# First loads in pieces, warm-up matmuls, a folded norm from half sums, masks by predicated copy, and the last unit by token half, in a two-block model kernel

## The reference

```python
def rmsnorm(x, g):
    y = x * rsqrt(mean(x * x, -1) + EPS)
    return y * g

def first_block(x, ...):
    for l in range(2):
        x = x + 0.5 * swiglu(rmsnorm(x, g_ffn1[l]), w1_a[l], w3_a[l], w2_a[l])
        x = x + mixer_1(rmsnorm(x, g_mix[l]))        # Fourier, convolution and pooling branches, gated
        x = x + 0.5 * swiglu(rmsnorm(x, g_ffn2[l]), w1_b[l], w3_b[l], w2_b[l])
    return rmsnorm(x, g_final)

def second_block(x, ...):
    for l in range(2):
        x = x + 0.5 * swiglu(rmsnorm(x, ffn1_norm[l]), ...)
        x = x + mixer_2(rmsnorm(x, mix_norm[l]))     # window attention and gated linear attention
        x = x + 0.5 * swiglu(rmsnorm(x, ffn2_norm[l]), ...)
    return x
```

## Time and profile before

| what | value |
|---|---|
| median of 3 runs | 2351.07 us |
| the profiled execution: its time, its span | 2351.17 us, 2349.4 us |
| PE busy | 2321.5 us, 99% |
| DVE busy, ACT busy | 1329.9 us (57%), 1119.6 us (48%) |
| mean granted TensorE clock | 0.999 |
| DMA | 417.06 MB, mean 178 GB/s |

### The profile page before, as it was taken

One profiled execution on the slowest core, in us unless ns is written; L12 is line 12 of the kernel. 1 busy time (PEld: TensorE's weight loads), 2 busy tenths in 40 slices (PEclk: granted clock), 3 DMA queues, 4 the chain that ended last, 5 costly groups with the idle time before them and its releaser, 6 DMA issues.

```text
span 2349.4 us, 26325 instructions
## 1 busy us (share of the span) xinstructions
PE 2321.5 (99%) x10836; PEld 1920.1 (82%) x10836; DVE 1329.9 (57%) x1456; ACT 1119.6 (48%) x1223; POOL 0.2 (0%) x4
## 2 busy tenths in 40 slices
PE   8999999999999999999999999999999999999999
PEld 6887888888888788888788888788888887878887
DVE  5554566555554466554555676755455548576553
ACT  5444444444444444443544664454454447545442
POOL 0000000000000000000000000000000000000000
PEclk9999999999999999999999999999999999999999
DMA  8555455555655455656556543455555555245653
GB/s 266 184 188 209 153 193 182 188 189 175 192 189 178 152 187 180 197 179 206 157 192 204 184 148 113 161 162 181 204 170 186 199 174 179 93 142 162 197 179 126
DMA packets 310268, 417.06 MB, mean 178 GB/s; under 512 B 16610, under 2 KB 201442, under 8 KB 310148
## 3 DMA queue, kind: packets, MB, share of 16 engines
q1 hardware_dynamic: 309860, 415.24, 54.1%
q10 hardware_dynamic: 288, 0.14, 0.0%
HBM read 414.27 MB, written 1.05 MB: 177 GB/s over the span
## 4 chain that ended last, share of the span: by engine, by line
PE 96%; DVE 2%; ACT 1%; issue 1%; DMA 0%; DVEq 0%; ACTq 0%
PE psum L587 30%; PE psum L589 29%; PE psum L588 29%; PE psum L604 3%; PE psum L858 1%; PE psum L684 1%; DVE wlo L1499 0%; ACT whi L1078 0%; PE psum L834 0%; PE psum L701 0%; PE psum L844 0%; PE psum L845 0%; PE psum L825 0%; DMA xt_in<-t_xt_dram 0%; DVE rb L1989 0%
## 5 line engine op out<-in xcount | busy, mean ns | idle before, releaser
L1499 DVE TENSOR_TENSOR wlo<-raw,whi 128x2048 fp32r<-128x2048 f32 (+2 forms) x408 | 882.5, 2183 | 459.3 <-ACT whi L1078 456.9
L1078 ACT ACTIVATE whi<-raw 128x2048 fp32r<-128x2048 f32 (+2 forms) x408 | 734.4, 1828 | 306.4 <-PE psum L589 301.7
L587 PE MATMUL psum<-whi,xt_hi 128*128 128x512 f32 (+1 forms) x2144 | 849.6, 396 | 10.0 <-DVE wlo L2026 10.0
L589 PE MATMUL psum<-whi,xt_lo 128*128 128x512 f32 (+1 forms) x2144 | 834.5, 389 | 0.0
L588 PE MATMUL psum<-wlo,xt_hi 128*128 128x512 f32 (+1 forms) x2144 | 833.4, 389 | 0.0
L587 PEld LDWEIGHTS psum<-whi,xt_hi 128*128 128x128 f32 x2144 | 404.0, 188 | 91.9 <-DVE wlo L2026 10.0
L589 PEld LDWEIGHTS psum<-whi,xt_lo 128*128 128x128 f32 x2144 | 403.3, 188 | 85.0
L588 PEld LDWEIGHTS psum<-wlo,xt_hi 128*128 128x128 f32 x2144 | 404.2, 189 | 79.7 <-issue 1.0
L587 PE MATMUL psum<-whi,ht_hi 128*128 128x512 f32 x704 | 275.3, 391 | 0.0
L589 PE MATMUL psum<-whi,ht_lo 128*128 128x512 f32 x704 | 274.1, 389 | 0.0
L588 PE MATMUL psum<-wlo,ht_hi 128*128 128x512 f32 x704 | 273.9, 389 | 0.0
(11 more groups left out here) (232 smaller groups left out, 1405.3 us busy)
## 6 DMA issues: line engine op xcount, KB each, us to landing
raw<-w_in_dram SPq DMA_DIRECT2D x180, 512.0 KB, 4.5
raw<-w_b_dram SPq DMA_DIRECT2D x128, 512.0 KB, 4.9
raw<-w_a_dram SPq DMA_DIRECT2D x126, 512.0 KB, 4.9
raw<-ffn_w_gate_dram SPq DMA_DIRECT2D x88, 512.0 KB, 4.1
raw<-ffn_w_up_dram SPq DMA_DIRECT2D x88, 512.0 KB, 5.2
raw<-ffn_w_down_dram SPq DMA_DIRECT2D x80, 512.0 KB, 4.7
raw<-w_o_dram SPq DMA_DIRECT2D x16, 512.0 KB, 4.4
raw<-w_proj_b_dram SPq DMA_DIRECT2D x16, 512.0 KB, 4.2
```

The costliest lines, as they stand in the source:

```text
L587: nc.tensor.matmul(pair(p, m)[:, out], hi[:, c, t], whi[:, slot, w], start=first, stop=False)
L589: last = nc.tensor.matmul(pair(p, m)[:, out], lo[:, c, t], whi[:, slot, w], start=False, stop=final)
L1078: nc.scalar.activation(whi[:, u % HL, first:n], raw[:, r, first:n], ACT.Copy).then_inc(hi_done, 1)
L1499: nc.vector.tensor_tensor(wlo[:, u % HL, first:n], raw[:, r, first:n], whi[:, u % HL, first:n], ALU.subtract).then_inc(w_ready, 1)
```

## The change

It has five parts.

1. xt comes in three pieces (chunks 0-1, 2-3, 4-7); the first half of unit 0 is split in two pieces of 512 columns, and PE starts after the first. Ahead of that, ACT runs one small Copy on a tile that DVE sets, and PE runs 16 transposes of `ident` into an unused bank once `ident` is in.
2. The norm between the blocks: x times gfin is kept as `xgf` (`x_scaled`), and the squares of x and of xgf are summed by column half (`final_squares`, results in `fss`), the first half during the last feed-forward of block 1. `final_norm` makes both scales from these sums. x = xgf * rfin is written afterwards. The load of `gfin` is issued in the middle of that feed-forward instead of at its end.
3. The masks: two `copy_predicated` into a zeroed `pg` in place of products and sums; `pg` is set to zero once in each mixer.
4. The last unit by token half (`last_blocks`): all six matmuls of tokens 0-127, then those of 128-255; DVE adds the first half after the semaphore `first_m`.
5. The wait for `ident` is made once, ahead of the warm-up, and not in each `hidden_transposes`.

```diff
+WARM = 16
+FIRST_PARTS = (slice(0, 2), slice(2, 4), slice(4, 8))
...
+                if (e.block, e.lay) == (1, LAYERS - 1) and u0 > 0:
+                    eng.wait_ge(w_used, units(e, u0, HL))
+                    eng.dma_start(gfin[:, :], a["g_final"].rearrange("(a n) -> a n", a=1).partition_broadcast(P)
+                                  ).then_inc(gfin_in, 16)
...
             xt_part(0)
             first_unit(a["w1_a"], a["w3_a"], 0, first_in)
             xt_part(1)
             first_unit(a["w1_a"], a["w3_a"], 1, raw_in[0])
+            xt_part(2)
             gate_up(flat(a["w1_a"]), flat(a["w3_a"]), 4 * P, 0, 1)
...
+            def last_blocks(u, p, split, chunks):
...
+                for m in range(MT):
+                    t = slice(m * P, (m + 1) * P)
+                    for i, c in enumerate(chunks):
+                        w = slice(i * 512, (i + 1) * 512)
+                        nc.tensor.matmul(pair(p, m), hi[:, c, t], whi[:, slot, w], start=False, stop=False)
+                        nc.tensor.matmul(pair(p, m), hi[:, c, t], wlo[:, slot, w], start=False, stop=False)
+                        last = nc.tensor.matmul(pair(p, m), lo[:, c, t], whi[:, slot, w], start=False,
+                                                stop=i == len(chunks) - 1)
+                    last.then_inc(first_m if m == 0 else w_used, 1)
...
             eng.sem_inc(w_used, HL)
+            eng.wait_ge(ident_in, 16)
+            for _ in range(WARM):
+                nc.tensor.transpose(psum[:, 5, 0:P], ident[:, :], ident[:, :])
             eng.wait_ge(first_ready, 1)
             eng.wait_ge(done, e.after(done, ("xt", "ffn0", 0, 0)))
-            blocks(0, 0, 0, XT, (0, 1), True, False, False, ready=False)
+            blocks(0, 0, 0, XT, (0,), True, False, False, ready=False)
+            eng.wait_ge(first_ready, 2)
+            blocks(0, 1, 0, XT, (1,), False, False, False)
...
+            def final_squares(half, scaled):
+
+                cols = slice(512 * half, 512 * half + 512)
+                src, out = (xgf, junk2) if scaled else (x, junk)
+                for m in range(MT):
+                    last = nc.scalar.activation(out[:, m, cols], src[:, m, cols], ACT.Square,
+                                                accum_out=fss[:, scaled, half, m:m + 1])
+                return last
...
                 if stage == "ffn0" and (e.block, e.lay) == (2, 0):
-                    squares("final", out)
                     root("final")
+                    root(stage)
                     split(u0 + 3)
-                    eng.wait_ge(done, e.after(done, ("x2",)))
-                    squares(stage, out)
-                    root(stage)
...
+                if stage == "ffn0" and (e.block, e.lay) == (2, 0):
+                    eng.wait_ge(x_whole, wholes(e))
+                    final_squares(1, 0).then_inc(acted, e.mark(acted, ("ss", "final")))
+                    eng.wait_ge(xgf_done, 2)
+                    final_squares(1, 1).then_inc(acted, e.mark(acted, ("ss", "ffn0")))
+                    x_hi(stage, 1)
...
+                        if next_stage == "ffn0" and (e.block, e.lay) == (1, LAYERS - 1):
+                            final_squares(0, 0)
+                            eng.wait_ge(xgf_done, 1)
+                            final_squares(0, 1)
...
+            def x_scaled(half):
+
+                cols = slice(512 * half, 512 * half + 512)
+                for m in range(MT):
+                    last = nc.vector.tensor_tensor(xgf[:, m, cols], x[:, m, cols], gfin[:, cols], ALU.mult)
+                last.then_inc(xgf_done, 1)
+
             def final_norm(u0):
 
-                norm("final", rfin)
-                split(u0 + 3)
-                eng.wait_ge(gfin_in, 16)
-                for m in range(MT):
-                    ins = nc.vector.scalar_tensor_tensor(out=x[:, m, :], in0=x[:, m, :], scalar=rfin[:, m:m + 1],
-                                                         in1=gfin[:, :], op0=ALU.mult, op1=ALU.mult)
-                ins.then_inc(done, e.mark(done, ("x2",)))
-                norm("ffn0", rstd)
+                for i, (stage, out) in enumerate((("final", rfin), ("ffn0", rstd))):
+                    eng.wait_ge(acted, e.after(acted, ("ss", stage)))
+                    e.link(nc.vector.tensor_tensor(ss[:, :], fss[:, i, 0, :], fss[:, i, 1, :], ALU.add))
+                    if i == 1:
+                        for _ in range(2):
+                            e.link(nc.vector.tensor_tensor(ss[:, :], ss[:, :], rfin[:, :], ALU.mult))
+                    mean_root(stage, ss[:, :], out)
                 ins = nc.vector.tensor_tensor(rstd[:, :], rstd[:, :], rfin[:, :], ALU.mult)
                 ins.then_inc(done, e.mark(done, ("rstd", "ffn0")))
+                split(u0 + 3)
+                for m in range(MT):
+                    nc.vector.tensor_scalar(x[:, m, :], xgf[:, m, :], rfin[:, m:m + 1], None, ALU.mult)
...
+                elif (e.block, e.lay) == (2, 0):
+                    eng.wait_ge(x_whole, wholes(e))
+                    x_scaled(1)
                 split(u0 + 2)
...
+                    for k in range(2):
                         lv = 2 * i + k
+                        mask = pairs[:, lv:lv + 1, :].bitcast(I32).broadcast_to([P, MT, P])
+                        level = bank(("weights", h, i))[:, 2 * k * P:2 * (k + 1) * P].rearrange("p (m t) -> p m t", m=MT)
+                        ins = nc.vector.copy_predicated(pg[:, :, :], mask, level)
+                        if k == 0:
+                            e.link(ins)
...
+                nc.vector.memset(pg[:, :, :], 0.0)
...
+            nc.vector.memset(rt[:, :], 1.0).then_inc(warm, 1)
```

More of the change, by code:

```diff
@@ L231, in build @@
         junk = sb(ffn, "junk", [P, MT, D])
+        junk2 = sb(ffn, "junk2", [P, MT, D])
         gfin = sb(ffn, "gfin", [P, D])
+        xgf = sb(ffn, "xgf", [P, MT, D])
         ffn.close()
@@ L327, in build @@
         vecs_in = semaphore("vecs_in")
-        xt_half_in = [semaphore(f"xt_half_in{i}") for i in range(2)]
+        xt_part_in = [semaphore(f"xt_part_in{i}") for i in range(3)]
+        warm = semaphore("warm")
+        first_m = semaphore("first_m")
         out_ready = semaphore("out_ready")
         folded = semaphore("folded")
+        xgf_done = semaphore("xgf_done")
         tables1_in = semaphore("tables1_in")
@@ L592, in blocks @@
                     last.then_inc(w_used, 1)
+            def last_blocks(u, p, split, chunks):
+                hi, lo = split
+                slot = u % HL
+                eng.wait_ge(w_ready, units(e, u, RAW))
+                for m in range(MT):
[7 more added lines that the diff above has]
+                    last.then_inc(first_m if m == 0 else w_used, 1)
             def wide(u, p, split, first=0, end=4):
@@ L675, in ffn_tensor @@
                     blocks(u + i, 0, 1, HT, range(4 * i, 4 * i + 4), False, False, True)
-                blocks(u + 5, 0, 1, HT, (20, 21), False, True, True)
+                if next_stage == "end":
+                    last_blocks(u + 5, 1, HT, (20, 21))
+                else:
+                    blocks(u + 5, 0, 1, HT, (20, 21), False, True, True)
             def mix1_tensor(u0):
@@ L1462, in _ @@
             eng.dma_start(vecs[:, 0:V_FOLDED], a["t_vecs"]).then_inc(vecs_in, 16)
+            eng.wait_ge(warm, 1)
+            nc.scalar.activation(ms[:, :], rt[:, :], ACT.Copy)
             eng.wait_ge(vecs_in, 16)
-            eng.wait_ge(xt_half_in[0], 16)
+            eng.wait_ge(xt_part_in[0], 16)
             first_hi_of(0, 0)
@@ L1467, in _ @@
             eng.wait_ge(w_used, 1)
-            nc.scalar.activation(whi[:, 0, 0:1024], raw[:, 0, 0:1024], ACT.Copy).then_inc(first_hi, 1)
+            for k in range(2):
+                cols = slice(512 * k, 512 * k + 512)
+                nc.scalar.activation(whi[:, 0, cols], raw[:, 0, cols], ACT.Copy).then_inc(first_hi, 1)
+            eng.wait_ge(xt_part_in[1], 16)
             first_hi_of(0, 1)
             split(0)
-            eng.wait_ge(xt_half_in[1], 16)
+            eng.wait_ge(xt_part_in[2], 16)
             first_hi_of(1, 0)
@@ L1549, in norm, with mean_root @@
                 eng.wait_ge(acted, e.after(acted, ("ss", stage)))
-                nc.vector.tensor_scalar(ms[:, :], ss[:, :], 1.0 / D, EPS, ALU.mult, ALU.add).then_inc(
+                mean_root(stage, ss[:, :], out)
+            def mean_root(stage, squares, out):
+                nc.vector.tensor_scalar(ms[:, :], squares, 1.0 / D, EPS, ALU.mult, ALU.add).then_inc(
                     done, e.mark(done, ("ms", stage)))
@@ L1644, in ffn_vector @@
                             half_done()
+                            if (e.block, e.lay) == (1, LAYERS - 1):
+                                eng.wait_ge(gfin_in, 16)
+                                x_scaled(0)
                     split(u0 + s + 3)
@@ L1798, in weights @@
                     eng.wait_ge(small, e.after(small, ("weights", h, i)))
```

(29 more changed lines are left out.)

22 lines of the change are left out of this document (11 added, 11 removed).

## The result

The changed kernel takes 2357.57 us (median of 10 runs, 2356.85 to 2357.67) against 2351.09 us of the kernel before (10 runs, 2351.03 to 2351.55) on the same chip: a ratio of 1.0027, with an interval of 1.0017 to 1.0036. It is 6.5 us slower where 9.6 us less was forecast. The profiled execution has a span of 2355.8 us, 6.4 more than before's.

The account below looks back on a forecast made before the run. TensorE, busy 99% of the span, was taken as the bound, so only its waits counted. Start, norm, masks and end summed as 0.0 - 4.75 - 4.4 - 0.5 = -9.65 us, giving 2341.5 us; range 2339.3 to 2345.8.

Parts of the forecast that it names:

- a dear copy: In the masks, a sign that the prediction is wrong: a predicated copy of 700 ns or more.
- a lower clock: On PE, a sign that the prediction is wrong: a clock below full after 17 us.
- D: Mixer masks: predicated copies near the reciprocal's price make DVE the bound, slower than before, at least 2356.7 us; chance 0.03.
- the end: Last unit: first addition and store lie beneath PE's last six matmuls, one store follows; -0.5 us, bounds -0.8 and -0.3.
- Start: Kernel start: PE begins earlier but then waits for loads and the first hidden tile; 0.0 us, bounds -0.3 and +1.6.
- rival C: Start: PE idles 2.8 us before unit 1 and the clock falls; net +1.5 us, 2343.0 us; chance 0.18.
- Rival A: Start: its gain counts in full, up to 3.4 us more, 2338.1 us; chance 0.07.
- Norm between the blocks: Between the blocks: the gap and slow matmuls behind it go, -5.1 us, a new wait adds 0.35; net -4.75 us.
- rival E: Between the blocks: the half-sum chain is longer than read, so half of the 5.1 us stays, 2344.0 us; chance 0.08.
- Masks: Mixer masks: 0.73 us off each of three PE waits in two layers; -4.4 us, bounds -7.0 and 0.
- B: Mixer masks: a predicated copy costs about twice as much, 0.69 us; -1.5 instead of -4.4, 2344.4 us; chance 0.17.

Follow-up runs that it names:

- the shorter spacer: The changed kernel with the unused tile `spacer` at SPACER = 48 instead of 56, putting tiles behind `fss` back at their old addresses: 2340.74 us, ratio 0.9956.

## Why the prediction was wrong

**The step that failed** is one that the sum left out. Part 2 was costed by its instructions and its DMAs, and the tile `fss` that it allocates was not costed at all, so the sum held -9.65 for what the change does and nothing for where the other operands then lie. That term is +16.8 us (the changed kernel with one spacer less the same kernel with the other). The text on what would make the prediction wrong named a dear copy and a lower clock; a matmul at full clock that is spaced 233 instead of 227 ns was not among them. None of the rivals had this mechanism either. D had the right sign for another reason, and its mark was absent: the predicated copy takes 445 ns, and DVE is busy for less time than before.

**The sum of the rest** was right to 0.8 us: 2341.5 forecast, 2340.74 measured with the operands where they were. Nearly all of the difference is one term, the end, which was mis-sized and lay outside its bound. Term by term:

*Start, forecast 0.0, in the changed kernel's trace +0.5, with the shorter spacer -0.3.* No run has part 1 alone, so this is read from where the first hidden tile is turned; the eleven traces of kernels with the old start have that between 29.43 and 29.81 us, so neither number is clear of the scatter by more than 0.3. The timeline of the changed kernel's start:

```profile
4.77 3.67 PE L1080 MATMUL psum<-ident 128*128 128x128 f32 x16 [4.77 <-DMA ident<-t_ident_dram]
8.13 0.56 PE L596 MATMUL psum<-whi,xt_hi 128*128 128x512 f32 x1
8.53 0.40 PE L597 MATMUL psum<-wlo,xt_hi 128*128 128x512 f32 x1
...
13.67 0.39 PE L598 MATMUL psum<-whi,xt_lo 128*128 128x512 f32 x1
17.35 0.47 PE L596 MATMUL psum<-whi,xt_hi 128*128 128x512 f32 x1 [3.29 <-DVE wlo L1551]
...
18.59 0.63 PE L598 MATMUL psum<-whi,xt_lo 128*128 128x512 f32 x1
19.02 0.63 PE L596 MATMUL psum<-whi,xt_hi 128*128 128x512 f32 x1
```

The first real matmul starts at 8.13, earlier than the 9.2 forecast (the transposes began at 4.77, where 5.6 was said) and 1.9 before the old 10.02, and its followers come 0.23 us apart where they came 0.43. Then all of it is given back, as forecast: PE is out of work at 14.1 us and waits for unit 1's wlo. Unit 2 is raised to whi at 18.54 after ACT waited 3.66 us for its load, against 18.75 and 3.68:

```profile
18.54 1.91 ACT L1109 ACTIVATE whi<-raw 128x2048 fp32r<-128x2048 f32 x1 [3.66 <-DMA raw<-w_a_dram]
```

In the windows of the changed kernel (stretch, its length, busy time and count of PE, PEld, DVE, ACT and POOL, granted clock, DMA share, GB/s) the fall of rival C is seen, 1.2 us after PE had resumed:

```profile
17.40:18.50 1.10, 1.10 (x5) 0.93 (x6) 0.00 (x0) 0.00 (x0) 0.00 (x0) 1.00 1.09 345
18.60:21.90 3.30, 3.30 (x9) 2.62 (x8) 1.42 (x1) 3.30 (x4) 0.00 (x0) 0.50 1.10 348
```

Half clock is 1.2 GHz, and eight matmuls at 0.43 us cost 8 x 0.20 = 1.6 us, not the 2.6 of thirteen. 1.1 us of it is covered by the slack in front of the first hidden tile, which is turned at 29.96 against 29.43, +0.5 where rival C said +1.5. Rival A falls: no start came 3.4 us earlier at this place. With the shorter spacer the idle time was 2.69 us, the clock stayed up, and PE met the wait in front of the hidden tile that was foreseen (0.52 us where 1.1 was said), at 29.11. Two executions with the same start code went both ways; the rule of the Trainium skill (TensorE: Matmul & The Clock Gate, "HAM oscillation — how this bites in real kernels") holds in the one and not in the other. The length of the idle stretch alone doesn't decide: the clock fell after 3.3 us here and after 1.8 us in the kernel without the warm-up, and not after 2.7. What does was not found.

*Norm between the blocks, forecast -5.1 + 0.35 = -4.75, measured -4.4 alone in the medians.* In the traces of the changed kernel, of the one with the shorter spacer and of this part alone, the clock doesn't fall there, the matmuls behind the gap start 5.1 us earlier than before, measured against those ahead of it, and the new wait takes 0.45 to 0.5: -4.6. After:

```profile
1124.63 0.64 ACT L1148 ACTIVATE junk<-x 128x512 f32<-128x512 f32 x1 [2.15 <-DVE x L1595]
...
1127.20 1.55 ACT L1121 ACTIVATE xt_hi<-psum,vecs 128x256 fp32r<-128x256 f32 x4
...
1128.06 1.66 DVE L1566 SCALAR_TENSOR_TENSOR xt_lo<-psum,vecs,xt_hi 128x256 fp32r<-128x256 f32 x4
...
1129.22 0.39 PE L598 MATMUL psum<-whi,xt_lo 128*128 128x512 f32 x1
...
1129.77 0.50 PE L596 MATMUL psum<-whi,xt_hi 128*128 128x512 f32 x1 [0.16 <-DVE xt_lo L1566]
...
1137.66 0.87 DVE L1675 SCALAR_TENSOR_TENSOR hid<-psum,rstd,gate 128x256 f32<-128x256 f32 x2
...
1140.81 0.60 PE L628 MATMUL psum<-ident,hid 128*128 128x128 f32 x4
1141.16 0.47 PE L596 MATMUL psum<-whi,xt_hi 128*128 128x512 f32 x1
```

x_hi starts 1127.20 - 1124.60 = 2.6 us after x is whole, where it was 1.87: 0.7 later, as worked out. The low part ends at 1129.72, and PE starts the matmul that needs it 0.55 us after the one before, where 0.23 is usual: a new wait of 0.32, forecast 0.35 (the matmul behind it is 0.1 late too). The hidden tile is ready at 1138.5, 2.3 us ahead of PE, where 0.6 us in hand were said, so rival E falls. Most of the difference is the rescaling of x, costed at up to 1.25 us for 1024 columns: it took 746 ns. The rule of the Trainium skill on fp32 tensor_scalar (VectorE: DVE Perf Modes, "The perf-mode tier table") agrees roughly: a tensor_tensor of 1024 columns takes 1.23 us, 1.65 times as long.

*Masks, forecast -4.4, measured -4.6 alone (-4.5 in the trace).* DVE's group by shape, and the timeline of the same place as the earlier trace rows:

```profile
L1878 DVE COPY_PREDICATED pg<-pairs,psum 128x256 f32<-128x256 int32 x64 | 28.5, 445 | 15.9 <-PE psum L884 14.6
```

```profile
1469.97 0.92 DVE L1878 COPY_PREDICATED pg<-pairs,psum 128x256 f32<-128x256 int32 x2 [1.86 <-PE psum L884]
...
1470.94 0.50 PE L870 MATMUL psum<-spans,loga_hi 128*128 128x512 f32 x1 [0.86 <-DVE pg L1878]
```

A copy costs 445 ns, forecast 420; a pass lasts 0.97 us instead of 1.67, and the wait fell from 1.55 to 0.86 us. Of the other two waits of a layer the one of 0.9 fell to 0.2 us and the shortest is gone, as forecast. Rivals B and D fall.

*End, forecast -0.5 with a bound of -0.8, measured -1.3.* The timeline of the changed kernel:

```profile
2351.28 0.69 DVE L1727 SCALAR_TENSOR_TENSOR x<-psum,x 128x512 f32<-128x512 f32 x1 [15.82 <-PE psum L614]
...
2352.00 1.73 SPq L561 DMA_DIRECT2D out_dram<-x  x2
...
2352.68 0.69 DVE L1727 SCALAR_TENSOR_TENSOR x<-psum,x 128x512 f32<-128x512 f32 x1 [0.71 <-PE psum L614]
```

I had counted only SP's shorter issue. That step shows as DVE's: its last addition ends 2353.37 - 2352.25 = 1.1 us after the start of the last matmul, before it was 2346.25 - 2344.54 = 1.7. The bound allowed 0.3 more for the last store having the DMA to itself, and it is 0.7: the span ends 2355.8 - 2353.37 = 2.4 us after DVE's end, before 2349.4 - 2346.25 = 3.15.

**It adds up.** With the shorter spacer PE's last matmul starts 9.4 us earlier than before, which is -0.3, -4.6 and -4.3 to within 0.2, and the end gives 1.3: 10.7 us of span; the medians differ by 10.5 us. In the changed kernel +0.5, -4.6 and -4.3 make -8.4, but its last matmul starts at 2352.25, 7.7 us later than before's, so 16.1 us are left for the 2880 displaced matmuls. The 0.8 between the two starts makes up the rest of the 16.8 above. A displaced matmul that would have waited anyway costs nothing, which may be why it isn't the full 18; that was not tested.

Two things stay open: why the distance counts, since no record shows what a matmul spends its time on; and which matmuls other than these (fp32 operands rounded to fp32r, 128 by 128 by 512) obey it. Those of 256 columns here did not.

## What to carry to other kernels

When a change allocates a tile, list which tiles move, and in a kernel that PE bounds compare the mean of each matmul group, and the spacing from start to start, as well as the waits: 6 ns on 2880 matmuls outweighed three real gains of 1 to 5 us. For matmuls like these keep stationary and moving operands a multiple of 256 bytes apart in the partition (put small tiles behind the large ones, or let a spacer round up), and test a suspected address effect by moving one tile, then all. A warm-up ahead of work that soon waits for loads brought nothing that could be measured.

## What the runs showed of the hardware

- A matmul with a moving operand of 512 columns of fp32r followed the one before after 227 ns when its two operands' addresses differed by a multiple of 256 bytes, and after 233 ns when they were 32, 64 or 128 bytes off. It cost 17, 34 and 49 us when ht and the mixers' tiles, xt, or all stationary operands were off, 0.7 to 2.1% of the kernel. Matmuls of 256 columns showed no such price (119.4 ns before, 117.8 to 120.8 displaced), and it was the same with DVE and ACT idle.
- Neither operand's own address counted: all of them 32 bytes further on gave 2351.21 us against 2351.14 (ratio 1.0001).
- The granted clock fell to 0.50 from 18.54 us on, 1.2 us after PE had resumed from an idle stretch of 3.3 us, and was back at 21.95. After one of 2.7 us it did not fall, and after one of 1.8 us it did (0.50 from 18.21 to 21.62), so the length of the stretch alone doesn't tell.
- A predicated copy of 128x256 fp32 numbers from PSUM, with an int32 mask in SBUF, took 445 ns, and a tensor_scalar of 1024 fp32 columns in SBUF 746 ns.
